# Two-block transformer kernel: diagonal gates in the last block, head norm inside the projection, and new orders in the attention and the scan

## What is computed

```python
def _diff_attend(q, k, v, lam, subln, lam_init):
    s = jnp.einsum('bqhjd,bkhjd->bhjqk', q, k).astype(jnp.float32) * (HEAD_DIM ** -0.5)
    p = jax.nn.softmax(s, axis=-1)
    a = (p[:, :, 0] - lam * p[:, :, 1]).astype(v.dtype)
    o = jnp.einsum('bhqk,bkhe->bqhe', a, v)
    o = rmsnorm(o, subln) * (1.0 - lam_init)
...
        o = _mha(q_row, jnp.concatenate([k_win, kc], axis=1), jnp.concatenate([v_win, vc], axis=1),
                 mask, bias)
...
        o = jnp.einsum('bhck,bhkv->bhcv', qc * jnp.exp(gc), s) + jnp.einsum('bhij,bhjv->bhiv', att, vc)
...
    contrib = (out[dest] * gate_sorted[:, None]).astype(h.dtype)
    return jnp.zeros((n_tok, d), h.dtype).at[tok_sorted].add(contrib)

```

## Time and profile before

| | us |
|---|---|
| median of the runs (lowest, highest) | 3529.85 (3528.49, 3533.06) |
| the profiled execution, its own time | 3529.11 |
| the span in its profile | 3527.3 |

### The profile page before, as it was taken

How to read it: one execution, slowest core, us unless ns; L and a number is a source line. 1 busy time by engine, 2 the same in 40 slices (tenths; PEclk the granted TensorE clock), 3 DMA queues, 4 the chain that set the end, 5 groups by cost and what they waited for, 6 DMA issues and landing times. The chain is left out here.

```text
span 3527.3 us, 46837 instructions
## 1 busy us (share of the span) xinstructions
PE 3268.6 (93%) x18680; PEld 2681.7 (76%) x18680; DVE 2269.5 (64%) x2972; ACT 1466.2 (42%) x1948; POOL 332.9 (9%) x214
## 2 busy tenths in 40 slices
PE   7998989999998998889999998889889989999996
PEld 5887768888887896778787868779667766777774
DVE  6467756656656317758776555575665357888885
ACT  5216723212122116633233343433433246777774
POOL 0020000000000000000000004321100013222221
PEclk8999989999999999999999999999989999999998
DMA  6550013453542221045654229211013249999993
GB/s 238 192 172 13 1 48 93 134 167 119 168 127 87 66 75 55 22 126 184 212 176 148 55 76 273 57 37 49 25 42 90 72 185 363 383 374 369 378 364 109
DMA packets 371656, 522.46 MB, mean 148 GB/s; under 512 B 19618, under 2 KB 313122, under 8 KB 345872
## 3 DMA queue, kind: packets, MB, share of 16 engines
q1 hardware_dynamic: 362112, 503.25, 42.6%
q0 software_dynamic: 9360, 16.72, 1.4%
HBM read 484.46 MB, written 51.90 MB: 152 GB/s over the span
## 5 line engine op out<-in xcount | busy, mean ns | idle before, releaser
L270 DVE TENSOR_TENSOR lo<-exp_raw,exp_hi 128x2048 fp32r<-128x2048 f32 x192 | 438.9, 2290 | 65.3 <-ACT exp_hi L3548 65.3
L3548 ACT CAST exp_hi<-exp_raw 128x2048 fp32r<-128x2048 f32 x192 | 366.5, 1913 | 113.5 <-PE exp_down_acc L265 50.0
L263 PE MATMUL ffn_acc<-normed_hi,up_w_hi 128*128 128x512 f32 (+1 forms) x1056 | 377.1, 357 | 11.3 <-DVE lo L589 6.1
L264 PE MATMUL ffn_acc<-lo,up_w_hi 128*128 128x512 f32 (+1 forms) x1056 | 376.4, 356 | 0.0
L263 PEld LDWEIGHTS ffn_acc<-normed_hi,up_w_hi 128*128 128x128 f32 x1056 | 199.5, 189 | 44.2 <-DVE lo L270 7.0
L421 DVE SCALAR_TENSOR_TENSOR aside_w<-aside_w,aside_c 128x1024 f32<-128x1024 f32 x176 | 209.2, 1221 | 26.5 <-DMA aside_w<-in_ada_t 19.8
L264 PEld LDWEIGHTS ffn_acc<-lo,up_w_hi 128*128 128x128 f32 x1056 | 199.7, 189 | 31.1
L263 PE MATMUL ffn_acc<-gated_hi,down_w_hi 128*128 128x512 f32 (+1 forms) x528 | 190.9, 362 | 15.3 <-DVE lo L270 15.1
L1238 ACT ACTIVATE conv<-ffn_acc,vecs 128x768 f32<-128x768 f32 (+1 forms) x88 | 73.2, 882 | 290.2 <-PE ffn_acc L265 290.2
L264 PE MATMUL ffn_acc<-lo,down_w_hi 128*128 128x512 f32 (+1 forms) x528 | 189.9, 360 | 0.0
L265 PE MATMUL ffn_acc<-normed_hi,up_w_lo 128*128 128x512 f32 (+1 forms) x528 | 188.6, 357 | 0.0
(11 more groups left out here) (620 smaller groups left out, 8751.7 us busy)
## 6 DMA issues: line engine op xcount, KB each, us to landing
exp_raw<-in_w_experts SPq DMA_DIRECT2D x192, 1024.0 KB, 9.0
aside_w<-in_ada_t SPq DMA_DIRECT2D x176, 512.0 KB, 6.2
up_w<-in_ffn_up SPq DMA_DIRECT2D x88, 512.0 KB, 5.2
x_rows<-dn_zero SPq DMA_DIRECT2D x42, 384.0 KB, 5.4
y_rows<-dn_zero SPq DMA_DIRECT2D x42, 384.0 KB, 5.3
ada_w<-in_ada_first SPq DMA_DIRECT2D x8, 1024.0 KB, 12.3
v<-in_ada_t SPq DMA_DIRECT2D x16, 512.0 KB, 6.4
down_w<-in_ffn_down SPq DMA_DIRECT2D x16, 512.0 KB, 3.9
```

The costliest lines, as they stand in the source:

```text
L263: nc.tensor.matmul(out, left[0], right[0], start=start, stop=False)
L264: nc.tensor.matmul(out, left[0], right[1], start=False, stop=False)
L270: return engine.tensor_tensor(lo, value, hi.bitcast(F32), ALU.subtract)
L3548: nc.scalar.copy(hi[slot(e, j)][:], raw[tile(e, j)][:]).then_inc(tile_hi[j], 1)
```

## The change

Four parts, independent of each other.

1. The block of the head norm is gone. Its steps (now the class `Heads`) stand at the head of `residual` for layer 0: the same squares, sums, reciprocal and root. The spreads use PSUM of the third output tile and of the totals; from the third head on, a head's spread stands between the products of the heads before it. VectorE scales in place and makes the low part; the high part is now ScalarE's. Five idle products stand between the sums and the wait for the root. The casts of two weight tiles stand between ScalarE's squares and its root.
2. In the neighbourhood attention TensorE makes the scores one step later and the values before the next step's first transposes; ScalarE takes the values and the three sets before it makes the next exponentials.
3. In the scan the low part of the next head's gates moves from VectorE to GpSimd, behind its `kd` product. The first step of the states moves to the second level, and the other three to the fifth, sixth and seventh.
4. At the end VectorE makes, before the gathered rows are there, eight diagonal 128x128 matrices of the gates (`end_shares`). TensorE multiplies the gathered rows by them (float32, 128x512) and adds both in PSUM. ScalarE's first multiplication and VectorE's multiply-and-add are gone; VectorE multiplies the sum in PSUM by the modulation. The four first idle products wait for nothing and the two later ones are gone.

```diff
+HEADS_IDLE = 5
...
+            if first:
+                first(c)
             pe.wait_ge(ready, c + 1)
...
+    def high(self, act, hi, c):
+        act.wait_ge(self.scaled, c + 1)
+        self.K.nc.scalar.copy(hi[:, c, :], self.src[:, c, 0:self.tok]).then_inc(self.rounded, 1)
...
+        for _ in range(HEADS_IDLE):
+            nc.tensor.matmul(self.idle, ident, self.K.consts[:, 0:512], start=True, stop=True)
+        pe.wait_ge(self.split, 1)
+        for c in range(2):
+            self.spread(pe, c, parts)
+
+    def spread(self, pe, c, parts):
+        row = self.rows[:, c:c + 1].broadcast_to([KD, P])
+        if c >= 2:
+            pe.wait_ge(self.scaled, c - 1)
+        for a, b in parts:
+            self.K.nc.tensor.matmul(self.spreads[c % 2][:, a:b], row, self.root_hi[:, a:b], start=True, stop=False)
+            last = self.K.nc.tensor.matmul(self.spreads[c % 2][:, a:b], row, self.root_lo[:, a:b], start=False, stop=True)
+        last.then_inc(self.spread_full, 1)
...
+            if heads:
+                heads.squares(act)
             for n in range(2, 4):
                 ring.high(act, n)
+            if heads:
+                heads.roots(act)
+                for c in range(KD):
+                    heads.high(act, hi, c)
...
             for c in range(KD):
-                nc.vector.tensor_copy(hi[:, c, :], src[:, c, 0:tok]).then_inc(hi_ready, 1)
-                dve.wait_ge(hi_ready, c + 1)
+                if heads:
+                    dve.wait_ge(heads.rounded, c + 1)
...
                 lo_of(nc.vector, lo[:, c, 0:tok], src[:, c, 0:tok], hi[:, c, :]).then_inc(src_split, 1)
+                if heads and c + 2 < KD:
+                    heads.scale(dve, c + 2)
...
                     turn(g - 1, 1)
                     turn(g - 1, 2)
-                if g + 2 < STEPS:
-                    scores(g + 2)
+                    if g + 1 < STEPS:
+                        scores(g + 1)
+                    values(g - 1)
                 if g < STEPS:
                     turn(g, 0)
-                if g >= 1:
-                    values(g - 1)
...
-                if g < STEPS:
-                    exps(g)
                 if g >= 2:
                     take_values(g - 2)
                 take(g - 1)
+                if g < STEPS:
+                    exps(g)
...
-                head_norm(K, o, KD, tok, o, 1.0 / P, EPS, [K.subln[:]] * KD, rs[:, 0])
...
+                if it + 1 < HEADS:
+                    raw, high, low = parts[it + 1]
+                    pool.wait_ge(gates_hi, it + 1)
+                    lo_of(nc.gpsimd, low, raw, high).then_inc(gates_lo, 1)
...
-                    if lev == 1 and it + 1 < HEADS:
-                        raw, high, low = parts[it + 1]
-                        dve.wait_ge(gates_hi, it + 1)
-                        lo_of(nc.vector, low, raw, high).then_inc(gates_lo, 1)
-                    if lev == EARLY:
+                    if lev == 1:
...
+                        step(1)
+                    if lev >= EARLY:
+                        step(lev - 2)
...
+            for t in range(NTX):
+                for k in range(TOPK):
+                    last = nc.vector.tensor_scalar(shares[:, k, t, :], ident, gate[:, k, t:t + 1], None, ALU.mult)
+                last.then_inc(shared, 1)
...
+            def mix(t):
+                pe.wait_ge(shared, t + 1)
+                for k in range(TOPK):
+                    pe.wait_ge(got[k][t], 16)
+                    for n in range(2):
+                        half = scaled[:, t, n * KD // 2:(n + 1) * KD // 2, :].rearrange("p n q -> p (n q)")
+                        last = nc.tensor.matmul(half, shares[:, k, t, :], rows[:, k, t, n * 512:(n + 1) * 512], start=(k == 0), stop=(k == TOPK - 1))
+                last.then_inc(mixed, 1)
...
+            idle(4)
+            for t in range(NTX):
+                mix(t)
+                if t >= 2:
+                    turn(t - 2)
+            for t in range(NTX - 2, NTX):
+                turn(t)
```

More of the change, by code:

```diff
@@ L772, in done, with multiply @@
         engine.wait_ge(self.acc_full[n % ACCS], n // ACCS + 1)
-    def multiply(self, pe, acc, chunks, ready, right, parts, between=None):
+    def multiply(self, pe, acc, chunks, ready, right, parts, between=None, first=None):
         nc = self.K.nc
@@ L1031, in residual @@
+def residual(K, src, w, gate_at, tok, early, extra, following=None, sums=None):
     nc = K.nc
@@ L1037, in residual @@
         acc = K.ps(ctx, "res_acc", [P, ACCS, 1024])
-        squares = Squares(K, ctx, tok, K.ps(ctx, "res_totals", [P, 1024]))
+        totals = K.ps(ctx, "res_totals", [P, 1024])
+        squares = Squares(K, ctx, tok, totals)
+        heads = Heads(K, ctx, src, tok, sums, EPS, K.subln[:], squares.room, totals, (acc[:, ACCS - 1, :], totals),
+                      acc[:, 0, 0:512]) if sums is not None else None
         ring = Ring(K, "res", [n % 4 for n in range(KD)], early, extra)
@@ L1064, in _ @@
         def _(pe):
-            ring.multiply(pe, acc, KD, src_split, lambda c, a, b: (hi[:, c, a:b], lo[:, c, a:b]), parts)
+            if heads:
+                heads.tensor(pe, parts)
+            ring.multiply(pe, acc, KD, src_split, lambda c, a, b: (hi[:, c, a:b], lo[:, c, a:b]), parts,
+                          first=lambda c: heads and c + 2 < KD and heads.spread(pe, c + 2, parts))
             squares.tensor(pe)
@@ L1837, in first_block @@
             extra = Ahead(K, ctx, "res", [P, KD, P], None, None, room=v)
-            residual(K, o, wo, 16, tok, ahead, extra, both)
+            residual(K, o, wo, 16, tok, ahead, extra, both, rs[:, 0] if i == 0 else None)
         with ExitStack() as ctx:
@@ L2827, in keep, with step @@
                                           B[:, 3 + u % 2, :].rearrange("p (c i) -> p c i", i=P)).then_inc(a_out, 1)
+            def step(st):
+                for d in range(2):
+                    c = steps_of(d)[st]
+                    fade = (egl[:, d, c - NTX:c - NTX + 1] if c >= NTX else
+                            egc[:, d, c * P + last_of(d):c * P + last_of(d) + 1])
+                    last = nc.vector.scalar_tensor_tensor(S[:, d, st + 1, :], S[:, d, st, :], fade,
+                                                          span(0, 3)[:, d * NT + c, :], ALU.mult, ALU.add)
+                last.then_inc(states, 1)
+                dve.drain()
             nc.vector.tensor_copy(before[:], strict).then_inc(before_ready, 1)
@@ L2868, in _ @@
                         dve.drain()
-                        for st in range(1, NT - 1):
-                            for d in range(2):
-                                c = steps_of(d)[st]
-                                fade = (egl[:, d, c - NTX:c - NTX + 1] if c >= NTX else
-                                        egc[:, d, c * P + last_of(d):c * P + last_of(d) + 1])
-                                nc.vector.scalar_tensor_tensor(S[:, d, st + 1, :], S[:, d, st, :], fade,
-                                                               span(0, 3)[:, d * NT + c, :], ALU.mult, ALU.add)
-                            dve.drain()
-                        dve.sem_inc(states, 1)
+                        step(1)
+                    if lev >= EARLY:
+                        step(lev - 2)
                 keep(it, LEVELS)
@@ L3740, in _ @@
             nc.scalar.activation(square[:, 0:1], floor[:], ACT.Sqrt)
+            act.drain()
             for t in range(NTX):
-                first_half(t)
-                if t >= 1:
-                    root(t - 1)
-                if t >= 3:
-                    take(t - 3)
-            root(NTX - 1)
-            for t in range(1, NTX):
+                root(t)
+                if t >= 2:
+                    take(t - 2)
+            for t in range(NTX - 2, NTX):
                 take(t)
```

157 lines of the change are left out of this document (66 added, 91 removed).

## The result

The changed kernel takes 3522.98 us (median of 20 runs, 3516.88 to 3529.0). The kernel before, on the same chip and in turn with it, takes 3533.51 (20 runs, 3525.22 to 3539.56). The ratio is 0.997, 95% interval 0.9963 to 0.9977: 10.5 us faster, with 8 to 13 in the interval. The forecast was 25 us and 3505. The sign is right, the size is not, and 3523 lies outside the range of 3495 to 3517. Part of the distance is the start: the three runs of before that the prediction had, 3529.85, lie 3.7 under the median of the 20.

What follows compares the result with a forecast made beforehand. Taken as bound by TensorE, busy nine tenths of the span, with changes paying where it waits. Terms -6.0 - 12.0 - 6.5 - 0.5 = -25.0 from 3529.1 gave 3504.1, as median 3505; 3495 to 3517 holds eight in ten.

Steps and rivals of the forecast that it cites:

- five spreads between the products: Head norm: five of eight spreads fall between TensorE's products, 0.64 us each, together 3.2 against the gain.
- The half clock, forecast as before: Start of the projection's products: clock taken as low again, with the same loss of 2.8 us.
- about 0.15 later: Neighbourhood attention: ScalarE's first copy waits for the moved transposes; 0.35 us a step gained, period 5.1.
- The prediction's own sign of being wrong: Wrong if neighbourhood period stays 5.4, TensorE waits for exponentials, or a stage between the four places grows over 2 us.
- The covers named for the exponentials: Neighbourhood attention: exponentials end 0.7 us before TensorE wants them; the maxima they need have cover 0.4.
- rival (e): Neighbourhood attention: the scores ring binds with one set fewer ahead, 26 us slower there, total 3543; chance 0.04.
- the wait of 2.16: Scan: VectorE's wait for TensorE's late product before the last mask; spreading the states moves that mask 3.45 us earlier.
- its ends: Last block, net -0.5 us: ends -2, and +3 if the first mixing runs at half clock and gathers land later.
- The bounds of part 2, -6 and -16: Neighbourhood attention, net -12.0 us: ends -6 (0.15 a step gained) and -16 (the whole 0.46).
- Rival (b): Neighbourhood attention gains nothing because transposes behind the values still find ScalarE at the exponentials: 3517; chance 0.12.
- rival (d): Neighbourhood attention and scan both gain nothing: 3523, no change to be measured; chance 0.06.

Runs made afterwards that it cites:

- the doubled copy of set 2: Changed kernel with ScalarE copying set 2 of the neighbourhood attention twice, first to a place nothing reads; one execution, the step stays at 5.36 us.
- four other traces with the old scan: Kernel before with only part 1 (two traces), only part 2, or only part 4 of the change; their scan block takes 140.0 to 140.6 us.
- the part alone: Kernel before with only part 4 (diagonal gates at the end): 3536.84 us, ratio 1.0005 (0.9996 to 1.0015).
- both traces that have it: Changed kernel with VectorE making GpSimd's low parts and qe (scan 1.3 shorter); the same plus nine idle products and mixings before turns: 3520.9 us, ratio 0.9963.

## Why the prediction was right and wrong, step by step

**Part 1**, -6.0 forecast, -4.6 in its block (-5.5 in the two profiled executions). The first product came a little before where it was put (468.5 for 469.3) and 4.2 after the first spread, not 5. The mis-sized term is the five spreads between the products: 0.64 each, 3.2 together, was forecast, and each costs 1.08 (3.18 for 2.10 a head), 5.4 together. The half clock, forecast as before, ended 3.5 behind the first product where it had been 5.8, which gives about 1 back. That the clock would be low again held; that the idleness is the reason isn't shown, as it also fell with nine idle products. That this term reaches the whole isn't shown.

**Part 2**, -12.0 forecast, -2.6 measured. This step failed, and it is most of the miss. The mechanism was the right one: the next set of transposes fills the wait, and delays the first copy, which set 2 needs. The delay was mis-sized.

The prediction said that the copy, 0.3 after the end of the values, would begin "about 0.15 later". It begins 0.63 after that end (1395.70 for 1393.54 + 1.53 = 1395.07), 0.32 later. The prediction charged the set with the 0.46 for which it holds TensorE up, but ScalarE waits for the set's last result. A set runs 0.66 from its start to its last end (the x4 row); here it starts 0.07 before the values end, and ScalarE begins 0.04 after the set's end, as it does each time it waits for a set. The chain behind the copy had no slack: set 2 began 0.14 behind the copy's end in the kernel before, and begins 0.14 behind it now.

TensorE also gained less than 0.46: from the start of set 2 to the end of the values it needs 4.00 for 4.39, or 0.39 less, since from the turn of the weights to the first value product it is now 0.42 (1393.12 to 1393.54) and was 0.32. So about 0.39 is saved and 0.30 lost a step, which leaves the 0.09 measured. (The forecast's own terms, 0.46 less 0.15, make 0.31 and not the 0.35 that it took.)

Thirty steps of 0.09 give 2.7 instead of 10.5. The first step gave its 1.7 (1.5 forecast). Two things took some back that the prediction had not looked at: where ScalarE and GpSimd split the next block's weights, two steps are long (6.32 and 6.09) and before only one (6.07), which is 1.1, and at the end, where the scores run out a step earlier in the kernel before, its last three steps are 4.76, 4.76 and 3.89 and the changed kernel's 5.36, 4.48 and 4.23. That is 0.66 more where 0.27 less was due, 0.9 together. In sum 2.7 + 1.7 - 1.1 - 0.9 make 2.4, for the 2.6 measured. The prediction's own sign of being wrong, a period that stays at 5.4, is what came. The covers named for the exponentials (0.7 and 0.4) were enough, as the doubled copy of set 2 shows, and no chain round the scores closed: rival (e) had no part in it.

**Part 3**, -6.5 forecast, -6.2 measured over all traces, -2.7 between the two first. The term was right: states -3.1 from the fifth level on (3.45 forecast), GpSimd +1.1 (1.3 forecast). It was right for the wrong heads, since the wait of 2.16 in the earlier trace rows stands at a low clock, and the third head of the same trace had waited 0.6 at full clock and had only that to give. The stretches before the two masks, in the kernel before (columns as in the earlier trace rows):

```profile
2539.00:2542.40 3.40, 3.40 (x13) 2.77 (x11) 1.32 (x4) 1.19 (x2) 0.00 (x0) 0.51 0.03 5
2571.00:2574.80 3.80, 3.01 (x20) 2.54 (x20) 3.17 (x8) 1.28 (x3) 0.00 (x0) 1.00 0.02 4
```

In three of the four other traces with the old scan all of the first three heads waited 2.0 to 2.2, and in the fourth the third waited 1.9. The split into states and GpSimd is read from the rows of one head; the two were not run apart.

**Part 4**, -0.5 forecast, -1.5 over all traces of the block, within its ends. The clock stayed high. In the whole the part alone showed no gain.

**Sum.** With 2.6 for 12.0 in part 2 and the others as measured the terms give 15, and the whole has 10.5 and 13.4. The bounds of part 2, -6 and -16, were no bounds: the lower one, 0.15 a step, had no row behind it. Rival (b) had 3517, for another reason. The measured 3523 is rival (d)'s number, but by luck: (d) had nothing from the scan, which gained 6.2 in its block. A further 3.7 is the median of three runs, which lay below that of the 20.

## What to carry to other kernels

An engine's wait is filled for free only by work that nobody on the way to the next wait needs first: walk the filled step through once more, and charge a filler with its whole run to the last result (0.66 here) where another engine waits for it, not only with the time for which it holds its own engine (0.46). Before a gain is read from a stage, see how that stage varies where nothing is changed in it: one trace against one trace misjudged the scan by 4 us in a block that three other traces would have put right. A product that runs beside another, as the first of the scores did here, costs nothing, so there is nothing to gain by moving it elsewhere.

## What the runs showed of the hardware

- GpSimd is held up by VectorE as well: its low part of 1024 columns took 3.10 when it began while VectorE's `kd` product was running, which ended 0.86 later (2506.90 for 2506.04), 2.41 in the first head and 2.34 each in the earlier trace rows.
- Where VectorE's part of a head became shorter, TensorE's stretch behind it became longer, in both traces that have it: 8.06 and 8.07 us for 6.44 between the second and third head, at a granted clock of 0.77.
- The same kernel has its stretches at half clock in different places from one execution to the next, and its time spans 20 us (3519.97 to 3540.24 in 33 runs of before on one chip), more than the whole change is worth. That the clock makes all of this span isn't shown.
- Idle products up to 0.6 us before the spreads moved the fall of the clock from 0.8 to 4.5 us behind the first spread, and didn't prevent it (one execution).
- A set of four 128x128 transposes holds TensorE up for 0.46 us and runs 0.66 us to its last end; ScalarE's copy of it began 0.04 us after that end, and TensorE's next set 0.14 us after the end of the copy that it waited for.
